# Building half of a gate matrix by accumulating scatters instead of one-hot products, in a hybrid decoder block

## The reference

```python
v1, i1 = lax.top_k(s1, 16)          # s1, s2: scores of the two halves of the query
v2, i2 = lax.top_k(s2, 16)          # against 128 keys each
comb = v1[..., :, None] + v2[..., None, :]
sc, pos = lax.top_k(comb.reshape(tokens, 8, 256), 16)
experts = e1 * 128 + e2             # e1, e2: the two key numbers of the pair
gate = softmax(sc)
act = gelu(einsum('thkd,td->thk', u[experts], x)) * gate
out = einsum('thk,thkd->td', act, v[experts])
```

## Time and profile before

| | |
|---|---|
| median of 3 runs | 4711.98 us (4708.87 to 4714.17) |
| the profiled execution's own time | 4713.71 us |
| its span, first to last instruction | 4712.1 us |
| mean granted clock of TensorE | 0.964 of full speed |
| busy: PE / PEld / DVE / ACT / POOL | 91 / 78 / 72 / 37 / 19 % of the span |

### The profile page before, as it was taken

One profiled execution on the slowest core, in us unless ns is written; L12 is line 12 of the kernel. 1 busy time (PEld: TensorE's weight loads), 2 busy tenths in 40 slices (PEclk: granted clock), 3 DMA queues, 4 the chain that ended last, 5 costly groups with the idle time before them and its releaser, 6 DMA issues.

```text
span 4712.1 us, 67213 instructions
## 1 busy us (share of the span) xinstructions
PE 4302.6 (91%) x23716; PEld 3667.5 (78%) x23716; DVE 3409.5 (72%) x6418; ACT 1727.1 (37%) x3205; POOL 916.3 (19%) x885
## 2 busy tenths in 40 slices
PE   6999999999899799899999888888778999999998
PEld 3668877777788587798999777778778788888886
DVE  6530057777477543489997999997566998888888
ACT  3221146556566432322224555554111222222222
POOL 0000000000244210000001333333554222222221
PEclk9999999999999899999999999999899999999999
DMA  6642123332666553322223555556889999999996
GB/s 250 236 171 94 48 86 134 128 122 91 195 189 189 192 185 101 108 88 83 80 91 114 208 208 206 206 206 254 298 315 317 312 303 299 289 289 289 289 289 203
DMA packets 487554, 913.53 MB, mean 194 GB/s; under 512 B 228722, under 2 KB 277250, under 8 KB 482548
## 3 DMA queue, kind: packets, MB, share of 16 engines
q1 hardware_dynamic: 385684, 534.58, 34.7%
q0 software_dynamic: 95840, 363.13, 21.8%
q10 hardware_dynamic: 5760, 12.59, 0.7%
HBM read 722.20 MB, written 187.97 MB: 193 GB/s over the span
## 4 chain that ended last, share of the span: by engine, by line
PE 25%; DVE 24%; DMA 6%; issue 2%; POOL 1%; ACT 0%; SPq 0%; DVEq 0%; ACTq 0%
PE ph_gate_ps L2440 14%; PE ph_hid_ps L2440 7%; DVE held_tiles L2751 5%; DMA ph_ring<-in_u_rows,held_tiles 5%; DVE ph_row_hot L2744 5%; DVE ph_ring L2737 3%; DVE held_tiles L2747 2%; PE ph_hid_ps L2365 2%; PE ph_hid_ps L2355 2%; POOL ph_ring L2323 1%; DVE ph_hot L2627 1%; DVE ph_hot L2634 1%; DVE ph_u_lo L2572 1%; DVE ph_score L2599 1%; DVE ph_index L2601 1%
## 5 line engine op out<-in xcount | busy, mean ns | idle before, releaser
L2365 PE MATMUL ph_hid_ps<-ph_n_hi,ph_u_hi 128*128 128x384 f32 x2048 | 720.9, 352 | 89.6 <-DVE ph_u_lo L2572 89.6
L2365 PE MATMUL ph_hid_ps<-ph_n_lo,ph_u_hi 128*128 128x384 f32 x2048 | 709.0, 346 | 0.0
L2365 PE MATMUL ph_hid_ps<-ph_n_hi,ph_u_lo 128*128 128x384 f32 x2048 | 708.0, 346 | 0.0
L2365 PEld LDWEIGHTS ph_hid_ps<-ph_n_hi,ph_u_hi 128*128 128x128 f32 x2048 | 405.2, 198 | 99.4 <-DVE ph_u_lo L2572 99.2
L2323 POOL DMA_INDIRECT ph_ring<-in_u_rows,held_tiles x256 | 319.4, 1248 | 777.0 <-DVEq L2660 578.0
L2737 DVE CUSTOM_DVE_ANT_0 ph_ring<-ph_ring,ph_n_rows 128x1024 f32<-128x1024 f32 x256 | 308.0, 1221 | 148.2 <-DMA ph_ring<-in_u_rows,held_tiles 147.4
L2365 PEld LDWEIGHTS ph_hid_ps<-ph_n_lo,ph_u_hi 128*128 128x128 f32 x2048 | 404.7, 198 | 0.2
L2365 PEld LDWEIGHTS ph_hid_ps<-ph_n_hi,ph_u_lo 128*128 128x128 f32 x2048 | 403.0, 197 | 0.0
L2341 POOL DMA_INDIRECT ph_ring<-in_v_experts,ph_pick_again x256 | 242.6, 948 | 765.9 <-DVE held_tiles L2837 734.1
L2522 ACT ACTIVATE held_tiles<-held_tiles 128x128 bf16<-128x128 bf16 x768 | 246.1, 390 | 281.6 <-DVE held_tiles L2747 277.3
L2837 DVE SCALAR_TENSOR_TENSOR held_tiles<-ph_ring,ph_factor,held_tiles 128x1024 f32<-128x1024 f32 x254 | 324.5, 1278 | 0.0
(11 more groups left out here) (395 smaller groups left out, 10339.5 us busy)
## 6 DMA issues: line engine op xcount, KB each, us to landing
ph_u_raw<-in_tiles SPq DMA_DIRECT2D x136, 512.0 KB
ph_v_raw<-in_v_experts SPq DMA_DIRECT2D x124, 512.0 KB
scratch_hidden<-ph_hidden SPq DMA_DIRECT2D x128, 384.0 KB
scratch_gate_tiles<-ph_gates SPq DMA_DIRECT2D x12, 4096.0 KB
ph_u_raw<-scratch_hidden SPq DMA_DIRECT2D x124, 384.0 KB
ph_hidden<-scratch_gate_tiles SPq DMA_DIRECT2D x124, 384.0 KB
proj_w_ch<-in_w_ch SPq DMA_DIRECT2D x49, 512.0 KB, 3.8
mb_w_raw<-in_w_branch POOLq DMA_DIRECT2D x48, 512.0 KB, 3.9
```

Of the source, the lines that this page charges most:

```text
L2365: mm = pe.matmul(hid_halves[r][:, c, :], u[r][a][:, k, :], n2[b][:, k, c * CUT:(c + 1) * CUT], start=(k == 0 and a + b == 0), stop=(k == K ...
```

## The change

The six dense tiles are split once more. Three (`DT = 3`, `GM = 384` tokens) still have their gates built from one-hots. For the other three (`ST = 3`, `SCATTERED = 384` tokens) GpSimd adds each weight straight into a DRAM tensor `scattered` of 16384 x 384 numbers, at the place expert x 384 + token. One such indirect DMA takes 128 weights, one per partition, with an add; there are 48 per head, 384 in all. GpSimd starts on a head when `head_done` says so and when the scatters of the head before have landed. From the sixth head on, one gather of a `u` row follows each scatter. A gather from the fifth on waits for a dot, so these late scatters lie between the gathers of the gate stage.

The tensor is first filled with zeros: 12 DMAs of 2 MB from an input, issued by ScalarE's queue in the projection, six in each of the first two turns, whose loop is unrolled for it.

The gate stage has 24 steps of two tiles and 16 tokens, still 48 tiles, so the tail keeps its 32. The low part of its tiles is made by VectorE. VectorE does three dots per half step from the fifth step on, 120 in the stage instead of 92, and four to five per tile in the tail. Six stores of 4 MB replace twelve; their tensor is now laid out by row, expert and token, so that a run is 64 tokens, 256 bytes. A gate tile of the expert stage is loaded in two DMAs, with runs of 1536 bytes, where one DMA had twelve runs of 256 bytes per partition. VectorE computes the places of the scatters in `experts_of`, in one more instruction per head; the expert and column numbers are now computed for three tiles only. The picks are transposed in three pieces.

The diff, cut to its core:

```diff
+        ZEROS = NK * NK * SCATTERED // (P * 4096)
+        d["scattered"] = nc.dram_tensor("scratch_scattered", (NK * NK * SCATTERED, 1), F32, kind="Internal").ap()
...
+                def clear(n):
+                    part = d["scattered"].rearrange("(c p n) a -> c p (n a)", c=ZEROS, p=P)
+                    act.dma_start(part[n], d["zeros"]).then_inc(zeroed, 16)
...
-
-                with act.Fori(0, TURNS - 1) as i:
+                        if n < CLEARS[i]:
+                            clear(sum(CLEARS[:i]) + n)
+
+                CLEARS = (6, 6, 0)
+                for i in range(TURNS - 1):
                     turn(i, OUTS[0][2], False)
                 act.wait_ge(dt_step, 1)
...
+                act.wait_ge(zeroed, 16 * ZEROS)
...
-TAIL_TILE0 = GATE_TILE0 + SM // 16
+
+
+ST = 3
+DT = MT - ST
+GM = DT * P
+SCATTERED = ST * P
+TAIL_TILE0 = GATE_TILE0 + 2 * (GM // 16)
...
-    d["gate_tiles"] = nc.dram_tensor("scratch_gate_tiles", (SM // GATE_TOK, NK, NK, GATE_TOK), F32, kind="Internal").ap()
+    d["gate_tiles"] = nc.dram_tensor("scratch_gate_tiles", (NK, NK, GM), F32, kind="Internal").ap()
+    scattered_rows = d["scattered"].rearrange("(p e n) a -> p e (n a)", p=NK, e=NK)
...
-        chosenT = held[:, 3:6, 0:SM]
+        chosenT = held[:, 3:6, 0:GM]
+
+        place_of = held[:, 5, S - SCATTERED:S].bitcast(U32)
+        place_of4 = place_of.rearrange("p (t h k) -> p t h k", t=ST, h=PH)
+        token = sp.sb("token", [P, ST])
...
                     j = 8 * k + (4 * s + x)
-                    m = GATE_TILE0 // 2 + 4 * k + (4 * s + x) // 2
-                    store(j + AHEAD, x % 2, m)
-                    load(j + (GATE_TILE0 + 4), x % 2, m + 2)
+                    m = GATE_TILE0 // 2 + 8 * k + (4 * s + x)
+                    for r in range(2):
+                        store(16 * k + (8 * s + 2 * x + AHEAD + r), r, m)
+                        load(16 * k + (8 * s + 2 * x + GATE_TILE0 + 4 + r), r, m + 2)
                     if x == STEPS - 1:
                         for b in range(NBANK):
                             sync.wait_ge(gates_taken[b], j + 2)
-                        sync.dma_start(d["gate_tiles"][2 * k + s], gates[s][:]).then_inc(gates_stored[s], 16)
+                        sync.dma_start(d["gate_tiles"][:, :, bass.ds((2 * k + s) * GATE_TOK, GATE_TOK)], gates[s][:]).then_inc(gates_stored[s], 16)
 
                 for s in range(2):
...
-                    sync.dma_start(to[2][r].rearrange("p (b n) -> p b n", n=GATE_TOK), d["gate_tiles"][:, :, bass.ds(e, 1), :].rearrange(
-                        "b p a n -> p b (a n)")).then_inc(gate_in[r], 16)
+                    sync.dma_start(to[2][r][:, 0:GM], d["gate_tiles"][:, bass.ds(e, 1), :].rearrange("p a n -> p (a n)")).then_inc(gate_in[r], 16)
+                    sync.dma_start(to[2][r][:, GM:SM], scattered_rows[:, bass.ds(e, 1), :].rearrange("p a n -> p (a n)")).then_inc(gate_in[r], 16)
...
+                def scatter(h, n):
+
+                    t, k = divmod(n, TOPK)
+                    at = t * P + h * TOPK + k
+                    pool.indirect_dma_start(d["scattered"], bass.IndirectOffsetOnAxis(place_of[:, at:at + 1], 0), held[:, 2, GM + at:GM + at + 1], None,
+                                            compute_op=ALU.add).then_inc(scattered[h], 16)
+
+                def gather(n):
                     if n >= NRING:
                         pool.wait_ge(dotted, n - NRING + 1)
                     pool.indirect_dma_start(ring[:, n % NRING, :], None, d["u_rows"], bass.IndirectOffsetOnAxis(
                         pick[:, pick_at(n):pick_at(n) + 1], 0)).then_inc(u_row_in[n % NRING], 16)
 
-                pool.wait_ge(head_done, PH)
-                for n in range(NRING):
-                    gather_first(n)
-                for j in range(SM // PER_STEP):
-                    r, m = j % 2, GATE_TILE0 // 2 + 1 + j // 2
-                    pool.wait_ge(u_hi[r], m + 1)
-                    pool.tensor_tensor(u[r][1][:], u_raw[r][:], u[r][0][:].bitcast(F32), ALU.subtract).then_inc(u_lo[r], 1)
-                    for n in range(picks_until(j), picks_until(j + 1)):
-                        gather_first(NRING + n)
-                for n in range(NRING + picks_until(SM // PER_STEP), PICKS):
-                    gather_first(n)
+                gathers = iter(range(PICKS))
+                for h in range(PH):
+                    pool.wait_ge(head_done, h + 1)
+                    if h >= 1:
+                        pool.wait_ge(scattered[h - 1], 16 * SCATTERS)
+                    for n in range(SCATTERS):
+                        scatter(h, n)
+                        if h >= PH - 3:
+                            gather(next(gathers))
+                for n in gathers:
+                    gather(n)
...
-                    tile(j % 2, (GATE_TILE0 + j) // 2)
                     for b in range(NBANK):
+                        if b % 2 == 0:
+                            tile(b // 2, GATE_TILE0 // 2 + j)
...
+                    own.of(dve.scalar_tensor_tensor(place_of4[:, :, bass.ds(h, 1), :].rearrange("p t a k -> p t (a k)"), placef[s][:, DT:MT, :],
+                                                    float(SCATTERED), token[:].unsqueeze(2).to_broadcast([P, ST, TOPK]), ALU.mult, ALU.add))
...
                 def step(j):
+
                     for b in range(NBANK):
+                        if b % 2 == 0 and j + b > 0:
+                            n = GATE_TILE0 + 1 + 2 * j + b // 2
+                            low(n % 2, n // 2)
                         dve.wait_ge(gates_mm[b], j + 1)
+                        toks = slice(j * PER_STEP + b * TOK, j * PER_STEP + (b + 1) * TOK)
                         dve.tensor_tensor(row_hot[b][:], iota[:].unsqueeze(1).to_broadcast([P, TOK, NK]),
-                                          chosenT[:, 0, slice(j * PER_STEP + b * TOK, j * PER_STEP + (b + 1) * TOK)].unsqueeze(2).to_broadcast([P, TOK, NK]), ALU.is_equal)
-                        toks = slice(j * PER_STEP + b * TOK, j * PER_STEP + (b + 1) * TOK)
+                                          chosenT[:, 0, toks].unsqueeze(2).to_broadcast([P, TOK, NK]), ALU.is_equal)
                         dve.tensor_tensor(col_hot[b], iota[:].unsqueeze(1).to_broadcast([P, TOK, NK]),
                                           chosenT[:, 1, toks].unsqueeze(2).to_broadcast([P, TOK, NK]), ALU.is_equal).then_inc(col_ready[b], 1)
                         dve.wait_ge(col_ready[b], j + 1)
                         for n in range(2):
                             ins = dve.tensor_tensor(term[n][b], col_hot[b], share[n][:, toks].unsqueeze(2).to_broadcast([P, TOK, NK]), ALU.mult)
                         ins.then_inc(hot_ready[b], 1)
-                    dots(picks_until(j + 1) - picks_until(j))
-
-                for j in range(SM // PER_STEP):
+                        if b % 2:
+                            dots(0 if j < 4 else 3)
+
+                for j in range(GM // PER_STEP):
                     step(j)
+                low((TAIL_TILE0 + 1) % 2, (TAIL_TILE0 + 1) // 2)
...
-                    dots(3 if y in FIRST_AT else 5 + (y < 14) if y < TAIL - 1 else PICKS)
+                    dots(3 if y in FIRST_AT else 4 + (y % 2 if y < 25 else 0) if y < TAIL - 1 else PICKS)
```

84 lines of the change are left out of this document (43 added, 41 removed).

## The result

The changed kernel takes **4532.55 us** in the median of 3 runs (4529.73 to 4541.16); the one before took 4711.98. The ratio of the means is 0.9624, with a 95% interval of 0.9602 to 0.9646. The profiled execution took 4529.73 us, with a span of 4528.1. The forecast was 4524, in a range of 4410 to 4650, so the total came out. Its reason for the new half step did not: the gate stage is held up by GpSimd's queue and not by the DMA work that the forecast named.

A forecast was written before the change was run, and what follows sets the result against it. The prediction took VectorE to bound the gate stage, with DMA expected next. Gate stage -152, tail -35 and small terms -1 summed to -188, giving 4524 us against the median, range 4410 to 4650.

The forecast's parts named there:

- VectorE as the bound before, and its relief: Gate stage: VectorE busy 686 of 695 us, 2.19 us per step lost to GpSimd blocking; afterwards 9.66 us per half step.
- The gate stage: DMA work sets 40 half steps at 11.6 us, TensorE the first 8 at 9.9: 543 us against 695, -152.
- on GpSimd I take a gather's issue, 0.93 to 1.99 us, median 1.03: Scatter issue on GpSimd priced as a gather's, plus 0.3 between two: six indirects 8.5 to 10.5 us per half step.
- Rival C: GpSimd becomes the bound, six indirects 13.7 us per half step: gate stage -68, tail -103, 4609 us; chance 0.16.
- The first five heads: Head stage: 48 scatters take 60 to 80 us per head, ending by 2502 us, before the first dot: no cost.
- A scatter's DMA work: 128 elements of 4 B, taken as 0.04 us per packet, 0.32 us per scatter; bounds 0.16 to 2.6.
- Rival D: Slower kernel through slow accumulating packets: break-even 0.24 us per packet, about 4830 us at 0.3; chance 0.13.
- The store's price: Gate stage: new store of 16384 packets of 256 B takes 20.9 us of DMA work instead of 12.3, six times.
- The tail: After the gate stage: 132 gathers instead of 160 and the last store, 355 us at DMA share 0.91, -35.
- The fills: Projection: 12 zero fills, 37 us of DMA work per burst of six, hidden: 0, bounds 0 to +40.
- The heads: Head stage: one more VectorE operation per head, 0.2 us for each of 8, +1.6 us.
- The expert stage: Gate loads go from 1536 to 256 packets, relieving DMA but not TensorE: 0, about 1056 us unchanged.

## Why the prediction was right, and where not

**VectorE as the bound before, and its relief: right.** row_hot is never held up again (min, median, max ns):

```profile
L2780 DVE TENSOR_TENSOR ph_row_hot<-ph_iota,held_tiles x96: 677/684/693, 2539.6 to 3082.7; 128x512 bf16<-128x512 f32 x96
```

In 429 us VectorE was busy 366.5, over 38 half steps 9.64 us each; the text had 9.66. How much of the -147 us comes from the end of the blocking alone wasn't tried.

**The gate stage: 543 forecast, 548 measured, for the wrong reason.** The first eight half steps, without dots, took 79.4 us, as forecast. For the other 40 the text took "11.6" from DMA work at a share of 0.92; they took 473, of which 18 is the late first dot and 11.37 each the rest. The step that failed is "on GpSimd I take a gather's issue, 0.93 to 1.99 us, median 1.03". A scatter that adds takes 1.86 us on average in this stage, and 1.55 at least. With 0.3 each between them six indirects take 11.3 us, not "8.5 to 10.5". Rival C rightly named GpSimd, but priced it at the longest issue of a gather, 13.7 us; the truth lay between. Its reason, the waits for VectorE's operation in progress, is part of it: the means of scatter and gather are 0.3 us each above their minima (1.55 and 0.94), 1.9 us in a half step. The add, which no rival had, is another 0.6 x 3 = 1.8 us. By this sum, an estimate, three pairs without either one would be at 9.5 us or less, under TensorE's 9.9.

That two sums agreed to 2% here, 11.6 and 11.37, is luck, and it hid the order of the bounds: without the stores' DMA work nothing changed, and with slower pairs on GpSimd the half step grew with them.

**The first five heads.** The text had 60 to 80 us per head and a cover that would be "gone if one takes over 2.2 us". From the first scatter at 2098.4 to the next head's at 2634.11 are 107 us per head, 2.2 us a scatter with the waits for landings. The cover was used up, and the first dot came 22 us late. The trace has the cause of the length in the same two terms: in the heads a scatter takes 1.92 us on average, 1.55 at least. "I am wrong if GpSimd has no idle time in the gate stage" is what happened.

**A scatter's DMA work.** Forecast 0.32 us. In the heads (2110 to 2480 us) 164 scatters were issued, and their queue's row is

```profile
q0 software_dynamic: 23328, 0.09, 17.5%
```

0.175 x 370 / 164 = 0.39 us; over 23328 packets on 16 engines that is 0.044 us per packet and engine, for the 0.04 taken. Rival D needed 0.24 and is out.

**The store's price.** For the strided store "20.9" us of DMA work was taken. In 400 us q1 took 169; tile loads and hidden stores, 32.2 MB, are 95 at the forecast's 340 GB/s, so a store is 18.6, an estimate. By the rule of the Trainium skill ("DMA: Bandwidth & Descriptors", why small descriptors are slow) the prediction's estimate was 16.9, nearly as far off on the other side. The sign of the term was wrong, though: the text booked the layout as a loss of 8.6 us per store, but the kernel with the contiguous one is 31 us slower in total. What counted wasn't the work but how long a gather waits beside it.

**The tail: 355 forecast, 351 measured**, at a share of 0.91 as taken. Late scatters still reach into its first 80 us, which the text didn't have, so part of the agreement may be luck.

**The fills: 0, right.** TensorE is busy 140 of 140 us. **The heads: +1.6 forecast, 0 measured.** The operation of the earlier trace rows stands at 2097.36 and 2157.39 in the first two heads, 60.0 us apart instead of 62.1, but that is one interval. From the first head's to the eighth's are 422.1 us after (2519.49) and 422.2 before (2524.31). Of the 8 us that came ahead of the gate stage 5 were there before the mixer: ScalarE's first copy of the queries starts at 1985.2 us instead of 1990.1. In the runs above it starts anywhere from 1984.7 to 1990.1, so this is spread between executions and no effect of the change. The other 3 lie between the heads and the gate stage, the "-3" of the text.

**The expert stage: 0 forecast, +9 measured.** The step that failed is "which relieves the DMA but not TensorE: 0". The DMA part was right (0.92 to 0.85). But the place of a buffer was no term of the sum at all, and it cost 16.60 us instead of 16.32 in every second pair of passes.

## What to carry to other kernels

Cost a queue that issues indirect DMAs by its instructions, not by its data alone. An indirect with an add took 1.55 us where a gather took 0.94. Where such a price is in no row, forecast the queue at both ends before a resource with a known price is named the bound. If two sums lie within a few per cent of each other, only an experiment that changes one and not the other tells which is the bound; here leaving out DMA work and adding GpSimd work did. Where small transfers that something waits for run beside a big store, look at their landing times and not only at the work: cutting a 4 MB store of 32 KB runs into 512 KB pieces of 4 KB runs gave 41 us here.

## What the runs showed of the hardware that was not expected

- An indirect scatter with an add takes at least 1.55 us of GpSimd's queue, the same without the add 0.96, a gather of u rows 0.94. Beside VectorE's work the first takes 1.86 on average in the gate stage and the last 1.25.
- A contiguous 4 MB store lands in 15.7 us, and gathers beside it land after up to 17.5 us. The same bytes in runs of 256 B take 29 us, and the gathers land after 9.0 us at the latest; in eight contiguous pieces 9.1.
- Products of TensorE with the same shapes and operands, back to back, were 1.7% slower (11.07 us instead of 10.88 for 48) in the turns whose weights lie in `n2` and `v1`, when the buffers allocated behind a constant of 8 or 12 bytes had moved; at 64 bytes 11.08. With the constant elsewhere they weren't. Why isn't known: most operands of the slow turns lie in `n2`, which had not moved; their last values and the buffers that are written meanwhile had.
